# ScalarE in place of VectorE for the scaling of the delta-rule chunks, with a re-parameterised plan, in a two-layer hybrid encoder kernel

## The chip, the cores and the metric

The kernel runs on one core of a Trainium2 chip. A core has TensorE (matrix products and transposes into the eight banks of PSUM), VectorE and ScalarE (element-wise work, both can read PSUM), GpSimd (element-wise work in SBUF), and SyncE, whose queue here issues almost all transfers. In the profile they are PE (PEld for its weight loads), DVE, ACT, POOL and SP. The metric is the device time of one execution in microseconds.

## What is computed

Two layers over a sequence of 1024 rows of 1024 values. Each layer projects the normalised input with one wide matrix, runs three groups of mixers on it, and projects their gated results back:

```python
h = rmsnorm(x, pre_norm)
proj = jnp.einsum('bld,de->ble', h, w_in)
(gq, gk, gv, gz, gb, ga, sx, sB, sC, sz, sdt, rq, rk, rv, rg) = split_cols(proj, IN_SIZES)
qkv = jax.nn.silu(causal_conv(jnp.concatenate([gq, gk, gv], axis=-1), gdn_conv))
o_a = rmsnorm(gated_deltanet(...), gdn_norm) * jax.nn.silu(gz)        # 4 heads of 128
o_b = rmsnorm(ssd(...) * jax.nn.silu(sz), ssd_norm)                   # 16 heads in 2 groups
o_c = rmsnorm(retention(...), ret_norm) * jax.nn.silu(rg)             # 4 heads of 128
out = jnp.einsum('ble,ed->bld', jnp.concatenate([o_a, o_b, o_c], axis=-1), w_out)
return x + rmsnorm(out, post_norm)
```

The change touches the gated delta rule. For each head and each chunk it solves a triangular system and carries a state:

```python
sol = lax.linalg.triangular_solve(a_low + eye, rhs, left_side=True, lower=True)
u, w = sol[..., :GDN_DV], sol[..., GDN_DV:]
v_new = u - jnp.einsum('bhcd,bhdv->bhcv', w, S)
o = q_exp_gcum @ S + attn @ v_new
S = S * jnp.exp(glast) + jnp.einsum('bjhd,bhjv->bhdv', kdec, v_new)
```

## The kernel before

**Parts.** The work is done in four parts (p = 0 to 3): layer 0 on rows 0 to 511, layer 0 on rows 512 to 1023, then layer 1 likewise. Chunks have 128 rows here, four to a part.

**Projections.** The columns of w_in are cut into 26 pieces of 256 columns (PIECES), in this order: gates of the delta rule (gz), its q, k and v (gdn), B and C of the state-space group (bc), its gates and inputs for two groups (sz and sx), and retention (ret). Each piece has two halves of eight slices; a slice is 6 matmuls of 256 columns or 3 of 512. Every product is made of three, since a weight w is kept as a rounded high part and a low rest: hi x hi, lo x hi, hi x lo. ScalarE makes the high part (L2131), GpSimd the low one (L2417), four steps "split" for each piece. In the parts 0 and 2 all pieces are split, and those that are not in AGAIN are also stored as their two parts in w_split ("keep"), to be loaded as such in the parts 1 and 3. The pieces in AGAIN (0 to 3) are loaded raw and split again there. Two pieces are in SBUF at a time (W_RING).

**The delta rule.** For each head: transposes and the gram matrix (gdn_turn, gdn_gram), a forward substitution in blocks of 16 on VectorE (gdn_base, 16 parts, L1836 to L1856), then doubling steps gdn_p and gdn_xx for levels 4 to 6, each in two halves: a product on TensorE, then VectorE masks it into PP (L1888) or subtracts it from X (L1875, L1878). Then, for each of the four chunks, in a strict chain:
- gdn_s: TensorE multiplies keys and queries with the state; VectorE makes the residual (L1898), ScalarE scales the query part (L2252);
- gdn_v: TensorE multiplies the inverse with the residual; VectorE scales the result by row, from PSUM into vhat (L1903; its PSUM bank is then free);
- gdn_o: TensorE makes the state's increment and the output; VectorE updates the state (L1909, L1913).
gdn_open (transposes of v, q k products) and gdn_x0 (L1864) stand ahead of the first chunk, and gdn_fin1 to gdn_fin3 behind the last one: a sum (L1920), a gate product (L1924), squares on ScalarE (L2258), their mean (L1930, L1674), a power on GpSimd (L2375) and the last gate product (L1941). Then mix_turn transposes the head's result for the output projection.

**Output projection.** The mixed columns form 4 groups (delta rule, two state-space groups, retention) with 4 units each, of two steps "out" with 24 matmuls. For the parts 0 and 2 a unit's weights are split by ScalarE (L2156) and VectorE (L1976). The out steps of group 0 exist from the transposition of head 3 on; a group's transposition (mix_turn) is placed only when no older out step is left.

**The plan.** make_plan writes the order of all steps before the kernel is built. It keeps a clock for each engine with fixed costs (ACT and DVE 300 ns for such small steps, SLICE 705 ns), plays the steps on it, and at each point takes what is due: first a side step, a transposition, the next mixing step, the next doubling step, the next step ahead. These are taken if they are due by now + NEAR. If none is, an out unit goes if the next projection is late or stuck or if the next mixing step is more than OUT_WAIT away and APART slices lie behind the last one; else the next projection slice goes. All engines run their share of this one list in order, with semaphores between them, so an instruction that waits holds everything behind it on its engine. SyncE's list of transfers is sorted by the place in the plan of the step that releases each.

**What a piece must wait for (frees).** A gate piece writes one of two gate buffers: sz(1,0) needs mix_turn of heads 0 and 1, sz(1,1) that of heads 2 and 3. sx(0,*) writes a slot that head 2 read: it needs gdn_open of head 2, and its last half also head 2's last gdn_p. sx(1,*) needs gdn_open of head 3, its last half head 3's last gdn_xx.

Of the kernel before, what the change touches and what calls it, by code (L numbers as in the profile page):

```python
# [19 lines left out]
ALU = mybir.AluOpType  # L20
ACT = mybir.ActivationFunctionType
# [3 lines left out]
P = 128  # L25
# [6 lines left out]
GH, SH, RH = 4, 16, 4  # L32
# [14 lines left out]
PC = 256  # L47
N_GDN_PC, N_GZ, N_BC, N_SZ, N_SX, N_RET = 6, 2, 2, 2, 2, 8
PIECES = ([("gz", 0), ("gdn", 0), ("gdn", 1), ("gz", 1), ("bc", 0), ("gdn", 2), ("bc", 1), ("gdn", 3),
           ("sz", 0, 0), ("gdn", 4), ("sz", 0, 1), ("gdn", 5), ("sz", 1, 0), ("sx", 0, 0), ("sx", 0, 1), ("sx", 1, 0),  # L50
           ("sx", 1, 1), ("sz", 1, 1)]
          + [("ret", i) for i in range(N_RET)])
AT = {piece: i for i, piece in enumerate(PIECES)}
# [5 lines left out]


NTH = {m: n for n, m in enumerate(m_of(piece, half) for piece in PIECES if piece[0] in ("gdn", "bc", "sx") for half in range(2))}
AGAIN = range(4)
W_RING = 2
Q = KD
SBUF = 224 * 1024 - 1
# [172 lines left out]
def make_plan():  # L238
# [120 lines left out]
    def play(step):  # L359

        k, p = step[:2]
        r = step[2:]
        after = needs(step)
        pe = lambda w: run("pe", w, *after, "banks")
        dve = lambda w, *e: run("dve", w, *e)
# [3 lines left out]
        def mark(name, time):  # L369
            at[name] = time  # L370
# [13 lines left out]
        elif k == "split":  # L384
            n, j = len(PIECES) * p + r[0], r[1]
# [22 lines left out]
        elif k == "proj":  # L408
            i, half, q = r
            n = len(PIECES) * p + i  # L410
# [75 lines left out]
        elif k == "gdn_p":  # L486
            h, lv, j = r
# [8 lines left out]
        elif k == "gdn_xx":  # L496
            h, lv, j = r
# [6 lines left out]
            act(300, "n")  # L504
        elif k == "gdn_v":
            mark("n", pe(LINE) + 100)
            mark(("vhat", p, *r), dve(300, "n"))
        elif k == "gdn_o":
            mark("n", pe(LINE) + 100)
            mark(("gdn_oo", p, r[0]), pe(LINE) + 100)  # L510
# [40 lines left out]
        elif k == "ssd_y":  # L551
            g, c = r
# [162 lines left out]
    while mix_at < len(mix) or inv_at < len(inv) or pre_at < len(pre) or front_at < len(front) or outs or turns or any(sides.values()):  # L715
# [10 lines left out]
        step = mix[mix_at] if mix_at < len(mix) and known(mix[mix_at]) else None  # L726
# [42 lines left out]
def emptied_by_act(step, tag):  # L769

    k = step[0]
    return (k in ("small", "small2", "cum_turn", "x_turn") or k == "gdn_p" and tag != step
            or (k, tag[-1]) in (("gdn_turn", "q"), ("gdn_s", "q"), ("bc_turn", 0), ("ret_turn", "k")))


# [5 lines left out]
GATE_WAIT = 0  # L781
TABLE_WAIT = 1500
NORM_WAIT = 3000
OUT_WAIT = 4000
LATE = 200
SPLIT_FROM = 6
APART = 16
KEEP = 2
RELOAD = 4400
HOLD = 250  # L790
NEAR = 0
AHEAD = 2000
FAR = 1e12
SLICE, LINE, TURN, UNIT, TABLE, MB, LANDING = 705, 224, 109, 24 * 119, 1283, 3300, 2000
# [94 lines left out]
def no_state(step):  # L889

    return step[1] % 2 == 0 and step[3] == 0
# [42 lines left out]
def hybrid_kernel(nc, x, w_in, w_small, w_out, cons, rope, pars, rows, post_norm, out):  # L934
# [15 lines left out]
    with ExitStack() as ctx:  # L950
# [47 lines left out]
        sc = sb("sc", 2, 4, NT)  # L998
# [18 lines left out]
        resid, vhat = wk[:, 11, 0:2], wk[:, 11, 2:4]  # L1017
# [18 lines left out]
        small = flat[:, 3072:3072 + NT * NSM].rearrange("p (t n) -> p t n", t=NT)  # L1036
# [41 lines left out]
        def bank(tag):  # L1078
            return ps[:, bank_of[tag], :]
# [4 lines left out]
        def wait_filled(eng, tag):  # L1084
            eng.wait_ge(filled[bank_of[tag]], use_of[tag] + 1)
# [4 lines left out]
        def empty(ins, tag):  # L1090
            ins.then_inc(emptied[bank_of[tag]], 1)
# [52 lines left out]
        for n in range(PARTS * len(PIECES)):  # L1144
            p, i = divmod(n, len(PIECES))
# [4 lines left out]
        for n in range(PARTS * NT):  # L1150
            p, t = divmod(n, NT)
# [505 lines left out]
        def _(dve):  # L1657
# [8 lines left out]
            tt, ts, stt = nc.vector.tensor_tensor, nc.vector.tensor_scalar, nc.vector.scalar_tensor_tensor  # L1666
# [20 lines left out]
            for s in plan:  # L1687
                k, p = s[0], s[1]
                l, first_half = p // 2, p % 2 == 0
                if k == "norm":  # L1690
                    t = s[2]
                    for j in range(2):
                        tag = (*s, j)
# [8 lines left out]
                elif k == "small_turn":  # L1702
# [10 lines left out]
                    a, e, z, q, r, m = v  # L1713
# [18 lines left out]
                elif k == "proj":  # L1732
                    i, half, q = s[2], s[3], s[4]
                    tag = s[:4]
# [154 lines left out]
                elif k == "gdn_s":  # L1889
# [5 lines left out]
                    else:  # L1895
# [1 line left out]
                        wait_filled(dve, tag)  # L1897
                        empty(stt(resid[:, c % 2, :], bank(tag)[:, 0:P], dec[:, 0, c, h:h + 1], vb[:, c, :],  # L1898
                                  ALU.mult, ALU.subtract), tag)
                elif k == "gdn_v":  # L1900
                    h, c = s[2:]
                    wait_filled(dve, s)
                    empty(ts(vhat[:, c % 2, :], bank(s)[:, 0:P], sc[:, (GH * p + h) % 2, 0 if no_state(s) else 1, c:c + 1], None,  # L1903
                             ALU.mult), s)
                elif k == "gdn_o":
                    h, c = s[2:]
                    wait_filled(dve, s)
# [168 lines left out]
        def _(act):  # L2076
# [20 lines left out]
            for s in plan:  # L2097
# [24 lines left out]
                elif k == "split":  # L2122
# [6 lines left out]
                    if j == 2:  # L2129
                        act.wait_ge(w_in_sem[n % W_RING][1], loads_done(n))  # L2130
                    A(w_hi[:, n % W_RING, j * 512:(j + 1) * 512], wr[:, n % W_RING, j * 512:(j + 1) * 512], ACT.Copy)\  # L2131
                        .then_inc(S["w_hi_ready"], 1)
                elif k == "mix_turn" and s[2] == 0:
                    wait_filled(act, s)
                    A(mixT_hi[:, s[3], :], bank(s), ACT.Copy).then_inc(S["mix_hi"], 1)
# [334 lines left out]
```

## Time and profile before

| | before |
|---|---|
| median of 3 runs | 2117.5 us (2117.46 to 2117.93) |
| the profiled execution | 2121.16 us |
| its span, first to last instruction | 2119.2 us |
| TensorE busy | 2040.7 us (96%) |
| VectorE busy | 1453.5 us (69%) |
| ScalarE busy | 897.6 us (42%) |
| GpSimd busy | 525.3 us (25%) |
| mean granted clock of TensorE | 0.992 |

An engine is busy from an instruction's start to its end; matmuls overlap, and their ends are modelled. "A <- B" in a list of waits means that A stood still until B had ended. The granted clock is 1.00 at 2.4 GHz and 0.50 at 1.2 GHz. The mean granted clock is over the whole span, so 0.992 is a few short stretches at half the clock.

### The profile page before, as it was taken

To read this page: it belongs to the slowest core of one execution; us is meant where nothing else is said; L and a number is where in the kernel's file an instruction comes from. 1 tells how busy PE (TensorE), PEld (TensorE's weight loads), DVE (VectorE), ACT (ScalarE), POOL (GpSimd) and SP (SyncE) were. 2 spreads that over 40 slices of the span, in tenths; PEclk is the share of its full clock that TensorE was granted. 3 is DMA by queue.
4 is the path that set the end of the run, shared out by engine and by line. 5 is a ranking of instruction groups with operands and counts; after the bars stand their busy time and mean duration, and the time that the engine had idled before them with its cause. 6 is when DMAs were issued, how large, how long until landed. Compare 5 with 4: busy or idle time off the path is not lost.

```text
span 2119.2 us, 38332 instructions
## 1 busy us (share of the span) xinstructions
PE 2040.7 (96%) x14628; PEld 1880.3 (89%) x14628; DVE 1453.5 (69%) x3428; ACT 897.6 (42%) x1805; POOL 525.3 (25%) x464
## 2 busy tenths in 40 slices
PE   7998899999999999999999998899999999999997
PEld 6887888999889988899889897799988999899997
DVE  5888877756688787734578887775466877766334
ACT  5544376433533336412454344663335433474011
POOL 3433243333200101201243334433331001121001
PEclk9999999999999999999999999999999999999999
DMA  4554275666444565344355537556646445653424
GB/s 164 206 200 179 92 256 200 218 239 239 160 159 133 189 211 198 134 150 143 120 208 199 199 130 255 208 189 241 237 156 207 150 140 187 212 181 136 160 102 187
DMA packets 93589, 385.42 MB, mean 182 GB/s; under 512 B 10656, under 2 KB 11744, under 8 KB 81632
## 3 DMA queue, kind: packets, MB, share of 16 engines
q1 hardware_dynamic: 92832, 382.56, 51.6%
q8 instruction: 118, 1.93, 0.4%
q14 instruction: 63, 0.52, 0.1%
q10 hardware_dynamic: 576, 0.41, 0.1%
HBM read 248.55 MB, written 134.38 MB: 181 GB/s over the span
## 4 chain that ended last, share of the span: by engine, by line
PE 78%; DVE 9%; DMA 5%; issue 4%; ACT 3%; POOL 2%; SPq 0%; POOLq 0%; DVEq 0%; ACTq 0%
PE ps L1355 74%; PE ps L1358 4%; DMA w_split<-w_low 1%; POOL w_low L2417 1%; DVE base L1849 1%; DVE base L1848 1%; DMA wo_split<-wo_parts 1%; DVE slot L1747 1%; DMA wo_loaded<-in_w_out 1%; DMA w_loaded<-in_w_in 0%; DMA wo_parts<-wo_split 0%; DMA xfin<-x_mid 0%; DVE bc L1747 0%; DVE acc L2073 0%; DVE acc L1747 0%
## 5 line engine op out<-in xcount | busy, mean ns | idle before, releaser
L1355 PE MATMUL ps<-w_hi,hT_hi 128*128 128x256 f32 x1792 | 526.8, 294 | 11.0 <-POOL w_low L2417 9.1
L1355 PE MATMUL ps<-w_hi,hT_lo 128*128 128x256 f32 x1792 | 504.1, 281 | 0.0
L1355 PE MATMUL ps<-w_low,hT_hi 128*128 128x256 f32 x1792 | 502.6, 280 | 0.0
L2417 POOL TENSOR_TENSOR w_low<-w_loaded,w_hi 128x512 fp32r<-128x512 f32 x240 | 328.9, 1388 | 508.5 <-ACT w_hi L2131 508.5
L1355 PEld LDWEIGHTS ps<-w_hi,hT_hi 128*128 128x128 f32 x1792 | 338.7, 189 | 19.5 <-POOL w_low L2417 11.8
L1355 PEld LDWEIGHTS ps<-w_low,hT_hi 128*128 128x128 f32 x1792 | 339.0, 189 | 5.4 <-issue 4.8
L1355 PEld LDWEIGHTS ps<-w_hi,hT_lo 128*128 128x128 f32 x1792 | 340.1, 190 | 0.0
L1355 PE MATMUL ps<-hT_hi,w_hi 128*128 128x512 f32 x768 | 318.6, 415 | 5.3 <-POOL w_low L2417 5.3
L1355 PE MATMUL ps<-hT_lo,w_hi 128*128 128x512 f32 x768 | 304.3, 396 | 0.0
L1355 PE MATMUL ps<-hT_hi,w_low 128*128 128x512 f32 x768 | 303.8, 396 | 0.0
L1355 PE MATMUL ps<-wo_parts,mixT_hi 128*128 128x256 f32 x960 | 269.3, 281 | 0.0
L1747 DVE SCALAR_TENSOR_TENSOR slot<-raw,par,slot 128x512 f32<-128x512 f32 x222 | 191.8, 865 | 21.1 <-ACT slot L2203 11.1
L1990 DVE TENSOR_TENSOR acc<-acc,ps 128x512 f32<-128x512 f32 x96 | 65.7, 687 | 180.4 <-PE ps L1355 173.8
L1355 PEld LDWEIGHTS ps<-wo_parts,mixT_hi 128*128 128x128 f32 x960 | 181.5, 189 | 2.3 <-issue 1.4
L2131 ACT ACTIVATE w_hi<-w_loaded 128x512 fp32r<-128x512 f32 x240 | 139.4, 621 | 87.7 <-DMA w_loaded<-in_w_in 87.6
L1355 PEld LDWEIGHTS ps<-hT_lo,w_hi 128*128 128x128 f32 x768 | 144.7, 188 | 33.6
L1355 PEld LDWEIGHTS ps<-hT_hi,w_hi 128*128 128x128 f32 x768 | 145.3, 189 | 32.5 <-POOL w_low L2417 5.6
L1355 PEld LDWEIGHTS ps<-hT_hi,w_low 128*128 128x128 f32 x768 | 145.4, 189 | 25.8
L1355 PE MATMUL ps<-wk 128*128 128x128 f32 (+2 forms) x992 | 156.2, 290 | 9.9 <-issue 3.2
L1355 PEld LDWEIGHTS ps<-wk 128*128 128x128 f32 x992 | 134.2, 193 | 29.6 <-issue 13.7
L1355 PE MATMUL ps<-wo_hi,mixT_hi 128*128 128x256 f32 x480 | 138.4, 288 | 3.5 <-DVE wk L1814 2.0
L1355 PE MATMUL ps<-wo_hi_odd,mixT_hi 128*128 128x256 f32 x480 | 136.9, 285 | 1.2 <-DVE wo_parts L1976 1.1
(224 smaller groups left out, 3846.1 us busy)
## 6 DMA issues: line engine op xcount, KB each, us to landing
w_loaded<-in_w_in SPq DMA_DIRECT2D x120, 512.0 KB, 5.0
w_split<-w_hi SPq DMA_DIRECT2D x44, 1024.0 KB, 7.9
w_split<-w_low SPq DMA_DIRECT2D x44, 1024.0 KB, 10.0
w_hi<-w_split SPq DMA_DIRECT2D x88, 512.0 KB, 5.8
w_low<-w_split SPq DMA_DIRECT2D x88, 512.0 KB, 7.0
wo_loaded<-in_w_out SPq DMA_DIRECT2D x32, 512.0 KB, 4.3
wk<-cum_rows SPq DMA_DIRECT2D x32, 512.0 KB, 3.9
wo_split<-wo_parts SPq DMA_DIRECT2D x32, 512.0 KB, 7.8
```

Of the source, the lines that this page charges most:

```text
L1355: return nc.tensor.matmul(o, a, b, start=start, stop=stop)
L1358: return nc.tensor.transpose(o, a, ident)
L1747: stt(o, r[:, j:j + HALF], w[:, j:j + 1], o, ALU.mult, ALU.add).then_inc(S["conv_done"], 1)
L1848: chain(tt(step_t[:, :, i + 1:], copy_of(h, i)[:, :, i + 1:], cols_x[:, :, i:i + 1].broadcast_to([P, NT, n]), ALU.mult))
L1849: chain(tt(cols_x[:, :, i + 1:], cols_x[:, :, i + 1:], step_t[:, :, i + 1:], ALU.subtract))
L1990: empty(tt(o, o, b, ALU.add), s)
L2131: A(w_hi[:, n % W_RING, j * 512:(j + 1) * 512], wr[:, n % W_RING, j * 512:(j + 1) * 512], ACT.Copy)\
L2417: tt(w_lo[at], wr[at], w_hi[at], ALU.subtract)\
```

## The change

The scaling of gdn_v goes from VectorE's program to ScalarE's, as a Copy with the same column as scale, and the planner is told so (the bank is emptied by ScalarE). The pieces sx(0,0) and sx(0,1) go ahead of sz(1,0). Piece 0 leaves AGAIN: it is stored in parts 0 and 2 and loaded as two stored parts in parts 1 and 3. OUT_WAIT goes from 4000 to 1e9 ns and NEAR from 0 to 250 ns. The plan that comes out differs in the order of the steps; the arithmetic is the same.

```diff
--- before.py
+++ after.py
@@ -47,7 +47,7 @@
 PC = 256
 N_GDN_PC, N_GZ, N_BC, N_SZ, N_SX, N_RET = 6, 2, 2, 2, 2, 8
 PIECES = ([("gz", 0), ("gdn", 0), ("gdn", 1), ("gz", 1), ("bc", 0), ("gdn", 2), ("bc", 1), ("gdn", 3),
-           ("sz", 0, 0), ("gdn", 4), ("sz", 0, 1), ("gdn", 5), ("sz", 1, 0), ("sx", 0, 0), ("sx", 0, 1), ("sx", 1, 0),
+           ("sz", 0, 0), ("gdn", 4), ("sz", 0, 1), ("gdn", 5), ("sx", 0, 0), ("sx", 0, 1), ("sz", 1, 0), ("sx", 1, 0),
            ("sx", 1, 1), ("sz", 1, 1)]
           + [("ret", i) for i in range(N_RET)])
 AT = {piece: i for i, piece in enumerate(PIECES)}
@@ -59,7 +59,7 @@
 
 
 NTH = {m: n for n, m in enumerate(m_of(piece, half) for piece in PIECES if piece[0] in ("gdn", "bc", "sx") for half in range(2))}
-AGAIN = range(4)
+AGAIN = range(1, 4)
 W_RING = 2
 Q = KD
 SBUF = 224 * 1024 - 1
@@ -504,7 +504,7 @@
             act(300, "n")
         elif k == "gdn_v":
             mark("n", pe(LINE) + 100)
-            mark(("vhat", p, *r), dve(300, "n"))
+            mark(("vhat", p, *r), act(300, "n"))
         elif k == "gdn_o":
             mark("n", pe(LINE) + 100)
             mark(("gdn_oo", p, r[0]), pe(LINE) + 100)
@@ -769,7 +769,7 @@
 def emptied_by_act(step, tag):
 
     k = step[0]
-    return (k in ("small", "small2", "cum_turn", "x_turn") or k == "gdn_p" and tag != step
+    return (k in ("small", "small2", "cum_turn", "x_turn", "gdn_v") or k == "gdn_p" and tag != step
             or (k, tag[-1]) in (("gdn_turn", "q"), ("gdn_s", "q"), ("bc_turn", 0), ("ret_turn", "k")))
 
 
@@ -781,14 +781,14 @@
 GATE_WAIT = 0
 TABLE_WAIT = 1500
 NORM_WAIT = 3000
-OUT_WAIT = 4000
+OUT_WAIT = 1000000000.0
 LATE = 200
 SPLIT_FROM = 6
 APART = 16
 KEEP = 2
 RELOAD = 4400
 HOLD = 250
-NEAR = 0
+NEAR = 250
 AHEAD = 2000
 FAR = 1e12
 SLICE, LINE, TURN, UNIT, TABLE, MB, LANDING = 705, 224, 109, 24 * 119, 1283, 3300, 2000
@@ -1897,11 +1897,6 @@
                         wait_filled(dve, tag)
                         empty(stt(resid[:, c % 2, :], bank(tag)[:, 0:P], dec[:, 0, c, h:h + 1], vb[:, c, :],
                                   ALU.mult, ALU.subtract), tag)
-                elif k == "gdn_v":
-                    h, c = s[2:]
-                    wait_filled(dve, s)
-                    empty(ts(vhat[:, c % 2, :], bank(s)[:, 0:P], sc[:, (GH * p + h) % 2, 0 if no_state(s) else 1, c:c + 1], None,
-                             ALU.mult), s)
                 elif k == "gdn_o":
                     h, c = s[2:]
                     wait_filled(dve, s)
@@ -2130,6 +2125,10 @@
                         act.wait_ge(w_in_sem[n % W_RING][1], loads_done(n))
                     A(w_hi[:, n % W_RING, j * 512:(j + 1) * 512], wr[:, n % W_RING, j * 512:(j + 1) * 512], ACT.Copy)\
                         .then_inc(S["w_hi_ready"], 1)
+                elif k == "gdn_v":
+                    h, c = s[2:]
+                    wait_filled(act, s)
+                    empty(A(vhat[:, c % 2, :], bank(s)[:, 0:P], ACT.Copy, scale=sc[:, (GH * p + h) % 2, 0 if no_state(s) else 1, c:c + 1]), s)
                 elif k == "mix_turn" and s[2] == 0:
                     wait_filled(act, s)
                     A(mixT_hi[:, s[3], :], bank(s), ACT.Copy).then_inc(S["mix_hi"], 1)
```

## Rows read from the trace of the kernel before

**Rows 1.** The page: span, then busy time, share, instructions.
```profile
span 2119.2 us, 38332 instructions
...
PE 2040.7 (96%) x14628; PEld 1880.3 (89%) x14628; DVE 1453.5 (69%) x3428; ACT 897.6 (42%) x1805; POOL 525.3 (25%) x464
```

**Rows 2.** Waits of PE: who <- for whom: total us, times, longest.
```profile
PE ps L1355 <- POOL w_low L2417: 14.4, 12, 3.1
...
PE ps L1358 <- DVE gate L1941: 6.8, 2, 5.5
PE ps L1355 <- DVE wk L1875: 4.6, 2, 4.0
PE ps L1355 <- DVE slot L1888: 4.5, 5, 2.0
...
PE ps L1355 <- DVE st_g L1913: 3.3, 2, 1.9
PE ps L1355 <- DVE wk L1898: 2.9, 1, 2.9
PE ps L1355 <- DVE wk L1903: 2.4, 3, 1.4
```

**Rows 3.** Windows, busy us: four delta-rule stretches; parts 0 and 2, then sum.
```profile
106.00:300.00 194.00, 177.71 (x1114) 156.84 (x1113) 161.81 (x446) 87.64 (x179) 69.10 (x55) 0.97 0.48 171
...
1143.00:1344.00 201.00, 182.59 (x1206) 163.55 (x1206) 167.12 (x422) 85.76 (x179) 76.92 (x62) 0.97 0.55 195
...
sum 754.00, PE 714.00 PEld 643.03 DVE 607.90 ACT 302.11 POOL 181.15; mean PE 178.50 PEld 160.76 DVE 151.97 ACT 75.53 POOL 45.29
```

**Rows 4.** Groups by form, DVE then ACT: busy us, mean ns | idle before.
```profile
L1903 DVE TENSOR_SCALAR wk<-ps,sc 128x128 f32<-128x128 f32 x64 | 22.2, 348 | 11.7 <-PE ps L1355 10.8
...
L2252 ACT ACTIVATE wk<-ps,dec 128x128 f32<-128x128 f32 x56 | 20.4, 364 | 81.5 <-PE ps L1355 80.9
```

**Rows 5.** Waits of PE between 190 and 222 us.
```profile
PE ps L1355 <- DVE wk L1875: 4.0, 1, 4.0
...
PE ps L1358 <- DVE wk L1864: 1.3, 1, 1.3
```

**Rows 6.** Windows of short stretches; PEclk stands after POOL's busy time.
```profile
217.20:220.60 3.40, 3.40 (x17) 3.40 (x17) 3.37 (x8) 0.60 (x1) 0.00 (x0) 0.50 0.00 0
...
1340.20:1347.00 6.80, 3.75 (x18) 3.75 (x19) 4.22 (x5) 6.77 (x18) 3.90 (x4) 0.50 0.02 8
...
1551.80:1555.20 3.40, 3.40 (x19) 3.40 (x18) 0.67 (x1) 2.46 (x6) 0.74 (x2) 0.50 0.00 0
```

**Rows 7.** Timeline of DVE and PE at 1342 us: start, us, instruction [idle before].
```profile
1341.70 1.50 DVE L1941 TENSOR_TENSOR gate<-gate,ss 128x512 f32<-128x512 f32 x1
...
1343.25 1.12 PE L1358 MATMUL ps<-con,gate 128*128 128x128 f32 x4 [5.47 <-DVE gate L1941]
```

**Rows 8.** Timeline of ACT and PE at the first piece of part 3.
```profile
1548.08 1.06 ACT L2105 ACTIVATE junk<-wk 128x1024 f32<-128x1024 f32 x1 [9.06 <-DMA wk<-x_mid]
...
1549.13 0.61 ACT L2131 ACTIVATE w_hi<-w_loaded 128x512 fp32r<-128x512 f32 x1
...
1551.42 0.38 PE L1355 MATMUL ps<-w_hi,hT_hi 128*128 128x256 f32 x1 [2.78 <-POOL w_low L2417]
```

**Rows 9.** Timeline: two chunks whose scaling came late on DVE.
```profile
167.80 0.46 PE L1355 MATMUL ps<-wk 128*128 128x128 f32 x2 [0.48 <-DVE wk L1878]
...
173.40 0.34 DVE L1903 TENSOR_SCALAR wk<-ps,sc 128x128 f32<-128x128 f32 x1
...
1777.37 1.70 ACT L2156 ACTIVATE wo_hi_odd<-wo_loaded,par 128x256 fp32r<-128x256 f32 x4 [8.33 <-DMA wo_loaded<-in_w_out]
...
1779.51 0.34 DVE L1903 TENSOR_SCALAR wk<-ps,sc 128x128 f32<-128x128 f32 x1
```

**Rows 10.** DMA issues: tensor, queue, count, KB each, median us to landing.
```profile
w_split<-w_low SPq DMA_DIRECT2D x44, 1024.0 KB, 10.0
```

## What the change does to the time, predicted

> **What bounds the kernel now.** The page comes first: TensorE is busy for 2040.7 us of a span of 2119.2 us [rows 1], and its total work isn't touched by the change. So the change can only act on the 78.5 us between (2119.2 - 2040.7), on gaps too short to be counted as idle, and on the clock. The second view says who holds TensorE up [rows 2]: GpSimd's low halves of the weights for 14.4 us, and VectorE for most of the rest, namely the gate product of L1941 (6.8 us) and the steps of the delta-rule chain (L1875 4.6, L1888 4.5, L1913 3.3, L1898 2.9, L1903 2.4 us). L1903 is the instruction that moves. The reader should see there that its own wait is 2.4 us in three places; all that the move can give beyond that comes from the room that it leaves on VectorE. The third view cuts out the four stretches in which the chain of the four delta-rule heads runs: VectorE is busy for 161.81 of 194 us in the first part of the sequence and 167.12 of 201 us in the third, 83% both, ScalarE for 45% and 43%, and TensorE idles for 16.3 and 18.4 us [rows 3]. That is where a VectorE instruction is worth something. In the other two parts the sum leaves TensorE only 5.3 us of idleness. The fourth view is the granted clock: three of the kernel's slow stretches, at half the clock (0.50, the 1.2 GHz level against 2.4 GHz), come right at the end of such a wait [rows 6].
>
> **The moved instruction.** 64 instructions at 348 ns leave VectorE: 22.2 us [rows 4]. The form that comes to ScalarE (Copy with a scale from a 128x1 operand, 128x128 out of PSUM) is there already as L2252, at 364 ns and without a table load: 64 x 0.364 = 23.3 us, on an engine with more than half of each stretch free. On the chain of a head each chunk gets 16 ns longer, 1.0 us in all if none is covered. The Trainium skill speaks against this edit: "ScalarE: Activation LUTs", section Rules for kernel authors, gives a multiply to VectorE, and its figure for an ACTIVATE with one 128x1 operand comes to 386 ns for 128 elements. By that the chain would grow by 64 x 38 ns = 2.4 us instead of 1.0 us; the row for the very form says 364 ns and decides.
>
> Waiting in line is the larger matter. On VectorE the scaling often waits behind other work: one matmul of this step began at 167.80 us, and its scaling at 173.40 us [rows 9]. On ScalarE it will stand behind conversions of weights, some of which wait for a transfer, with the gate and convolution evictions of the next projection behind it in turn; if it comes late, they do, and through them the two banks of the projections. At 1777.37 us ScalarE had sat 8.33 us waiting for a transfer, and VectorE, waiting for ScalarE's result, reached the scaling at 1779.51 us only [rows 9]: in such a place neither engine is the better one. I take the time in line as equal, with 5 us less or more as bounds. What is left is the room on VectorE: 22.2 of 607.9 busy us, 3.7% [rows 3]. The waits for L1888, L1913, L1898 and L1903 add up to 13.1 us [rows 2]; nothing is gone if each is a matter of order, 6.5 us if half is a matter of load. I take a fifth, -2.6 us, with the 1.0 us above: **-1.6 us**.
>
> **The order of the pieces.** Today sz(1,0) comes before sx(0,0) and sx(0,1). It writes the ring of gates that head 1's result leaves only with its turn (frees), so projections stop until head 1 is done. In the first part no out units exist yet to fill in, and TensorE waits 1.3 us for L1864 and 4.0 us for L1875 [rows 5]. Right after it comes a stretch at half the clock from 217.2 to 220.6 us in which TensorE is busy throughout: 1.7 us lost [rows 6]. sx(0,0) needs only gdn_open of head 2, and L1864 reads what that step wrote, so both waits lie behind it: after the change sx(0,0) can fill them, with 16 slices of the planner's 705 ns, 11 us of matmuls. Its convolution puts VectorE work into the same place, which delays the chain, but covered by projections. **-7.0 us**; bounds 0 (the stop moves to the next blocked piece) and -7.0.
>
> **The end of head 3 in the third part.** Here the last gate piece sz(1,1) waits for head 3: TensorE stands 5.47 us at 1343.25 us for L1941, which ends the chain of head 3 [rows 7], and then runs at half the clock up to 1347 us, with 3.75 us of busy time in that window, 1.9 us of it lost [rows 6]. The reordering doesn't add work to fill this place with; only a shorter chain does. 16 scalings of this part take 5.6 us off VectorE, about the size of the wait, but not all of them are on the path. Half: **-3.7 us**, bounds 0 and -7.4.
>
> **Piece 0 is split once (AGAIN).** In parts 1 and 3 the first piece is loaded as stored halves. Eight conversions on ScalarE and eight subtractions on GpSimd fall away. In part 3 this removes a wait: ScalarE sat 9.06 us for x_mid, the conversion queued behind it began at 1549.13 us, and TensorE went on at 1551.42 us after 2.78 us [rows 8], then at half the clock until 1555.2, 1.7 us [rows 6]. **-4.5 us**. Part 1 has no such wait. What is added: in parts 0 and 2 two stores of 1 MB after the first piece, and in parts 1 and 3 twice the bytes of the load. A store lands after 10.0 us [rows 10], and the load into the same ring slot has to wait for it, with everything behind it in SP's queue. Bounds: 0 and +5 us (half of a store, for each of two parts 2.5 us). I take 0, since the store is issued one half piece ahead of the load's own release and the slot's next piece is used one piece later.
>
> **NEAR from 0 to 250.** The planner may now put a chain step where its data is due up to 250 ns later, instead of one more slice of projection (705 ns) before it. A step whose due time falls anywhere in the last slice is brought forward in 250/705 = 0.355 of the cases and TensorE then waits 125 ns on average. Chain steps: 96 of gdn_p and as many of gdn_xx, 64 each of gdn_v and gdn_o, 56 of gdn_s, 64 of ret_o and 32 of ssd_y, 472 in all, counts by the loops, with those of gdn_v (L1903) and gdn_s (L2252) in [rows 4]. 472 x 0.355 x 0.125 = 20.9 us if each stands behind a slice. Many follow another chain step directly, so I take less than half, **+9 us**. Bounds +0 and +21. The gain in return (each chain a little earlier) is in the terms above. OUT_WAIT at 1e9 lets out units go only where projections are late or stuck or no mixing step is known; it saves them as filler for the stops and costs nothing by itself: 0, bounds -3 and +3.
>
> **Sum.** -1.6 - 7.0 - 3.7 - 4.5 + 9.0 = -7.8 us. The profiled execution took 2121.2 us, of which 2119.2 are span; it would take 2113.4. The median of the plain runs is 3.7 us lower, and 2117.5 - 7.8 = 2109.7 us.
>
> **Rivals.**
> (1) The stops move. The filling work is the same in all; projections used up beside head 1 are missing beside head 3, and the 7.0 us come back at sz(1,1) of the first part. For it: that is what the third part shows at 1343 us. Against it: in the first part sz(1,1) isn't delayed today. 2109.7 + 7.0 = 2116.7 us.
> (2) Slower: the slots opened by NEAR become waits. The planner charges 300 ns for the scaling, where rows show 348 and 364 ns [rows 4], and likewise for its neighbours, so a step put 250 ns before its planned due time waits for more than that. Place: everywhere a chain step stands behind a slice, in all four parts and in the retention steps too, where nothing is won. Price 20.9 us in place of 9, and 2.5 us more for the stores in each of two parts, against gains of 16.8 us without the half of the third part's 3.7: 2117.5 + 20.9 + 5 - 15.0 = 2128.4 us at the worst, 2123.4 without the stores. It decides from 16.8 us on, that is a mean wait of 36 ns over the 472 steps (I take 19).
> (3) VectorE's load is the true bound of the stretches with 83%: the third part's wait goes whole (-7.4), half of the 13.1 us goes too (-6.5 + 1.0), and NEAR costs half (+4.5): 2117.5 - 7.0 - 7.4 - 4.5 - 5.5 + 4.5 = 2097.6 us.
> (4) It doesn't do what it says: excluded for the move itself, which is one instruction for another; for OUT_WAIT it may be so, since it matters only where a mixing step is known and over 4 us off.
>
> **How the numbers follow.** Forecast (2103 to 2113): 0.48. Rival (3): 0.12. Rival (1) and everything else that ends within 0.2% (4.2 us, about what a measurement of this kernel can tell from no change): 0.22. Rival (2): 0.18. So faster 0.60, same 0.22, slower 0.18. The range goes from rival (3) to between the two values of rival (2): 2097 to 2126; below it I leave 0.06 and above it 0.08.
>
> **What the profile after would show.** ScalarE has 64 more instructions near 364 ns and VectorE 64 fewer; VectorE's busy time falls from 1453.5 us [rows 1] to about 1431. No waits for L1864 or L1875 around 210 us and no slow clock at 217 us. No wait for GpSimd's w_low at the first piece of part 3. The wait for L1941 in part 3 halved or gone. TensorE's waits, in number, rise (many of 0.1 to 0.3 us, "issue" or VectorE). Wrong if: a wait of over 3 us for L1941 stands in the first part (rival 1), the many small waits add up to over 17 us (rival 2), or new waits for the scaling on ScalarE, behind conversions that wait for transfers, exceed the 2.4 us that TensorE waits for it on VectorE.

## The result, and the profile after

The changed kernel takes 2147.2 us (median of 4 runs, 2143.98 to 2151.15) beside 2117.5 us: 1.0136 times as long, interval 1.0123 to 1.0149. That is 30 us slower, outside the range and on the other side of the forecast.

The page of the profiled execution after (span 2146.3 us), answering to [rows 1]:

```profile
PE 2054.7 (96%) x14628; PEld 1884.4 (88%) x14628; DVE 1430.0 (67%) x3364; ACT 911.7 (42%) x1859; POOL 510.1 (24%) x456
```

Work has moved as forecast: VectorE is at 1430.0 us (1431 forecast), with 64 instructions fewer. TensorE's matmuls are the same, and its busy time is 14 us longer. Its waits after, answering to [rows 2] (engine <- for whom: total us, times, longest; the lines behind the edit have moved up by one to five, so L1936 is L1941 of before):

```profile
PE ps L1355 <- issue: 20.6, 5, 9.4
PE ps L1358 <- DVE gate L1936: 9.8, 2, 5.0
...
PE ps L1355 <- DVE slot L1888: 8.0, 5, 3.2
PE ps L1355 <- POOL w_low L2416: 6.6, 9, 2.2
PE ps L1355 <- DVE wk L1875: 3.2, 5, 1.3
...
PE ps L1355 <- ACT wk L2131: 2.8, 2, 1.9
```

GpSimd's halves, 14.4 us before, cost 6.6; the moved scaling (L2131 now) costs 2.8 us where it had cost 2.4. New is the first row, 20.6 us of "issue", 17.6 us of it in two stops, of 8.2 and 9.4 us. Here is the first, in the timeline of PE, ACT and SP at the end of part 0 (start, us, instruction, [idle before <- releaser]):

```profile
513.31 2.04 PE L1355 MATMUL ps<-wk 128*128 128x128 f32 x8 [8.19 <-issue]
```
```profile
508.94 1.06 ACT L2100 ACTIVATE junk<-wk 128x1024 f32<-128x1024 f32 x1 [12.09 <-DMA wk<-in_x]
...
511.04 1.15 ACT L2104 ACTIVATE wk<-wk,xrs 128x1024 f32<-128x1024 f32 x1 [0.95 <-POOL xrs L2352]
512.09 0.36 ACT L2220 ACTIVATE slot<-ps 128x256 f32<-128x256 f32 x1
512.35 0.37 ACT L2221 ACTIVATE gate<-ps 128x256 f32<-128x256 f32 x1
512.62 0.60 ACT L2314 ACTIVATE wk<-ps 128x512 f32<-128x512 f32 x1
```
```profile
490.13 0.32 SPq L1288 DMA_DIRECT2D w_hi<-w_split  x1
490.49 0.43 SPq L1289 DMA_DIRECT2D w_low<-w_split  x1
490.97 0.43 SPq L1288 DMA_DIRECT2D w_hi<-w_split  x1
491.44 0.43 SPq L1289 DMA_DIRECT2D w_low<-w_split  x1
491.92 0.67 SPq L1297 DMA_DIRECT2D wo_split<-wo_hi  x1
492.63 0.64 SPq L1298 DMA_DIRECT2D wo_split<-wo_parts  x1
493.31 0.58 SPq L1292 DMA_DIRECT2D w_split<-w_hi  x1
493.93 0.63 SPq L1293 DMA_DIRECT2D w_split<-w_low  x1
497.06 1.21 SPq L1232 DMA_DIRECT2D wk<-in_x  x2
```

Read them from the bottom. SyncE issues 2 MB of the stored piece 0 (its halves; before, 1 MB raw), then four stores (two of 0.5 MB to wo_split and two of 1 MB to w_split, 3 MB together), and only then two tiles of x for part 1. ScalarE has reached the squares of such a tile and waits 12.09 us. In line behind it stand two evictions and the copy of the last retention head's keys (L2314, done at 513.2). TensorE's next matmuls, ret_s(0,3), read that copy. So "issue" stands here for a wait two steps away: TensorE waits for ScalarE, and ScalarE for a transfer. The same picture stands at the start of part 3: 13.34 us of waiting for x_mid on ScalarE, 9.44 us on TensorE at 1568.86. The clock fell in both. The rows of windows (length, PE, PEld, DVE, ACT, POOL busy, PEclk, DMA share, GB/s):

```profile
510.33:513.70 3.37, 0.39 (x2) 0.42 (x3) 0.00 (x0) 2.66 (x5) 0.59 (x2) 0.50 0.54 216
513.70:517.16 3.46, 3.46 (x19) 3.46 (x18) 0.69 (x1) 2.31 (x4) 0.74 (x2) 0.50 0.01 2
1561.60:1571.80 10.20, 2.94 (x14) 2.97 (x15) 0.69 (x1) 5.42 (x10) 1.49 (x4) 0.50 0.54 189
```

Outside the first and last 20 us, the clock is at 0.50 for 27 us before and for 44 us after. The waits of 190 to 222 us [rows 5] are gone, but at the end of head 3 there is now a stop in part 0 as well as in part 2 (timeline of PE, two places):

```profile
298.79 1.12 PE L1358 MATMUL ps<-con,gate 128*128 128x128 f32 x4 [4.97 <-DVE gate L1936]
```
```profile
1352.61 1.12 PE L1358 MATMUL ps<-con,gate 128*128 128x128 f32 x4 [4.83 <-DVE gate L1936]
```

A sum over all matmul records, worked out for this text, sorts the delays. For the first matmul of each step other than a projection or an out unit, I take the time since the matmul before it began, less the usual time for such a pair (the tenth percentile of all kernels' records of it at full clock). The last column is the time at a granted clock of 0.50 outside the first and last 20 us:

| kernel | delays under 1 us, sum | over 1 us, sum | at 0.50 |
|---|---|---|---|
| before | 10.8 us | 25.9 us | 27 us |
| after | 22.3 us | 46.7 us | 44 us |
| after with NEAR 0 (e2_near0, below) | 12.4 us | 30.2 us | 48 us |
| after with late stores (f3_stores_late) | 21.9 us | 30.5 us | 24 us |

These sums depend on what is called usual. A second count, with the usual time taken apart for each pair of steps and of tiles, gives 9.7, 22.5, 9.4 and 22.2 us under 1 us and 25.5, 44.5, 27.7 and 28.3 us over it. By that count the short delays are 19 to 25 us in all six kernels of this document with NEAR at 250, and 6 to 14 us in all fourteen with NEAR at 0.

### The profile page after: what moved, and what is told of

It is laid out like the page before. It is cut to its first block and busy times, and to the rows that moved or that the text cites. A ratio compares the mean times of both kernels' runs of the same rounds, so it can differ in the third digit from the quotient of the medians.

```text
span 2146.3 us, 38311 instructions
## 1 busy us (share of the span) xinstructions
PE 2054.7 (96%) x14628; PEld 1884.4 (88%) x14628; DVE 1430.0 (67%) x3364; ACT 911.7 (42%) x1859; POOL 510.1 (24%) x456
## 5 line engine op out<-in xcount | busy, mean ns | idle before, releaser
L2416 POOL TENSOR_TENSOR w_low<-w_loaded,w_hi 128x512 fp32r<-128x512 f32 x232 | 316.9, 1382 | 477.6 <-ACT w_hi L2126 477.4
L1747 DVE SCALAR_TENSOR_TENSOR slot<-raw,par,slot 128x512 f32<-128x512 f32 x222 | 186.2, 840 | 21.7 <-ACT slot L2204 10.0
L1355 PE MATMUL ps<-wk 128*128 128x128 f32 (+2 forms) x992 | 159.7, 294 | 29.6 <-issue 20.6
```

Source lines behind the costliest of these rows:

```text
L1355: return nc.tensor.matmul(o, a, b, start=start, stop=stop)
L1747: stt(o, r[:, j:j + HALF], w[:, j:j + 1], o, ALU.mult, ALU.add).then_inc(S["conv_done"], 1)
L2416: tt(w_lo[at], wr[at], w_hi[at], ALU.subtract)\
```

## The experiments

Each is a change of before or after. Where a setting of the planner is changed, the plan comes out anew; where it says so, the plan is kept. A ratio is to the kernel before as measured beside the run (medians from 2118.9 to 2119.3 us), with its 95% interval. Where two runs are compared in us, the difference is that of their medians, and each median is good to some 2 us, with four executions to 4.

### Which part costs

**after with AGAIN as before.**
```diff
-AGAIN = range(1, 4)
+AGAIN = range(4)
```


> The changed kernel with AGAIN back at pieces 0 to 3, the plan made anew. Theory A: piece 0 is loaded raw again, 1 MB instead of 2 MB ahead of the x tiles at the start of parts 1 and 3; the two waits shrink to what the kernel before shows (0 and 2.8 us), 2125 to 2131 us. If the x tiles' place in ScalarE's order alone makes the wait, it stays near 2147. Theory B and C: 2147 within 4 us (plus or minus what another plan gives).

2136.1 us, 1.0082 of before (1.0063 to 1.0100): 11 us faster than after, where theory A had 16 to 22. The two long stops are 3.9 and 2.9 us.

**after with NEAR as before.**
```diff
-NEAR = 250
+NEAR = 0
```


> The changed kernel with NEAR back at 0, the plan made anew. Theory B: the many small waits go, 2147 - 20 = 2127 us or less. Theory A: only as far as ret_s of head 3 is placed later; the waits under 0.25 us sum to little in the trace of the changed kernel (about 3 us more than before), so 2140 to 2147 us.

2116.4 us, 0.9987 (0.9977 to 0.9998): 31 us faster than after, in theory B's range. The two long stops are gone, and the small delays are back at 12.4 us. The clock is at 0.50 for 48 us here, as long as in after, so the 31 us aren't the clock's.

**after, its plan kept, scaling back on VectorE** (the branch of gdn_v goes back to VectorE's program, with the same bank order).

> The changed kernel with its plan unchanged, the 64 scalings alone moved back to VectorE. Theory C (ScalarE delays them): 2147 - 15 to - 25 us. Theory A and B: 2147 within 4 us; slower by up to 5 us if the room on VectorE was worth something.

2163.5 us, 1.0211 (1.0196 to 1.0227): 16 us slower than after: theory C is refuted, and the loss is more than the 5 us that the other theories allowed. TensorE's first row of waits in this run:

```profile
PE ps L1355 <- DVE wk L1903: 21.0, 17, 3.1
```
So the move is a gain on this plan, and what after loses against before isn't ScalarE's doing.

**before with NEAR 250 and nothing else.**

> The kernel before with NEAR at 250 in place of 0 and nothing else, the plan searched anew. Theory 1 (the allowance is the part that costs, by itself, with VectorE scaling as in before): 15 to 35 us slower than before, 2132 to 2152, and many small waits for VectorE, as in the run with the scaling moved back (20 us of waits on the scaling's line). Theory 2 (the allowance costs only together with the second kept first piece, whose transfers stand before the x tiles): within 5 us of before, since the kernel before keeps no first piece. The long stop ahead of ret_s(0,3) near 510 us tells too: under 1 us by theory 2, over 4 us by theory 1.

2144.1 us, 1.0114 (1.0098 to 1.0130), 25 us. No long stop at 510 us, so the size is that of theory 1 and the sign of the stop that of theory 2. The small delays are 21.1 us. Stops of 6.6 us at 219 and 4.0 at 1794 us are new, and one of 3.1 us at 1305 has grown to 4.4 at 1307. NEAR needs no other edit to cost 25 us. The two long stops of after aren't there, so on this plan the 25 us must be the short delays and other stops.

### What the two long stops are made of

**after, one step of ScalarE moved.** The scaling of x tile 2 is placed behind ret_turn(p,3), the step of which L2314 is ScalarE's part.
```diff
+    for p in (0, 2):
+        for step in (("rescale", p + 1, 2), ("scale", p + 1, 2)):
+            plan.remove(step)
+            plan.insert(plan.index(("ret_turn", p, 3)) + 1, step)
```


> The changed kernel with its own plan, except that in parts 0 and 2 the squares and the scaling of the next part's third x tile stand behind ret_turn of head 3 instead of ahead of it, so that ScalarE makes the key copy for ret_s before it waits for that tile. Theory A (ScalarE waits 12 us for an x tile whose load stands behind 5 MB of other transfers, and ret_s of head 3 stands behind it): the two PE waits of 8.3 and 9.6 us go, with the slow clock behind them, 2147 - 18 - 4 = 2125 us, or a few us more if the third tile's own norm is late then. Theory B (NEAR costs 20 us everywhere) and theory C (the scaling waits in line on ScalarE): within 3 us of 2147.

2134.9 us, 1.0077 (1.0060 to 1.0093), 12 us faster than after, where theory A had 22. The stops shrink to 2.0 and 3.5 us and stand now at norm, the step that needs the tile itself.

**after, the plan kept, stores behind the x tiles** in SyncE's list.
```diff
-                loads.append((where["proj", p, i, 0, Q - 1], n, ("keep", p, i)))
+                at = where["proj", p, i, 0, Q - 1]
+                if i == len(PIECES) - 1:
+                    at = max(at, where["norm", p + 1, 1] + 0.5)
+                loads.append((at, n, ("keep", p, i)))
```
(and likewise for the "keep_unit" that falls there)

> The changed kernel; on SyncE's queue the stores of kept weights that stand ahead of the loads of x tiles 2 and 3 of parts 1 and 3 (3 MB at each of the two places) are issued behind these two loads; the plan and all engines' orders stay. Theory 1 (the two long stops are the transfer of the x tile behind the kept data, which holds ScalarE's order and with it the evictions behind it): both stops shrink by what the stores took, 4 to 8 us each, so 8 to 14 us faster than after, 2133 to 2139. Theory 2 (the x tile's own load is long, whatever is ahead, or the load of the next first piece, which stays ahead, is what it waits for): under 3 us faster than after, and the waits of ScalarE for the x tile stay near 12 us.

2129.7 us, 1.0060 (1.0039 to 1.0081), 17.5 us faster than after (by the two ratios 16 us, good to 5), at or above the upper end of theory 1's 8 to 14. SyncE and ScalarE at the same place:

```profile
497.10 1.21 SPq L1238 DMA_DIRECT2D wk<-in_x  x2
498.35 0.43 SPq L1303 DMA_DIRECT2D wo_split<-wo_hi  x1
```
```profile
501.77 1.06 ACT L2106 ACTIVATE junk<-wk 128x1024 f32<-128x1024 f32 x1 [4.88 <-DMA wk<-in_x]
```
The load is issued at the same time (497.10 and 497.06), and the tile is used 7.2 us earlier (501.77 and 508.94). Four stores, 3 MB together, are all that was taken from ahead of it. Between 497 and 508.9 us the transfers of after moved 396 GB/s, by which 3 x 1048576 bytes take 7.9 us, an estimate. The Trainium skill ("DMA: Bandwidth & Descriptors", section Where 436 GB/s comes from) puts SBUF's sixteen ports together at 435 GB/s and says that the memory's side, about 358 GB/s for a core, binds for transfers between HBM and SBUF; by these figures the 3 MB take 7.2 or 8.8 us, both estimates. The trace's 396 GB/s is above the second figure, and the 7.2 us measured are nearest to the first. The windows of the place show what it was worth (TensorE busy of 20 us, first after, then this run):

```profile
1555.00:1575.00 20.00, 10.56 (x80) 10.39 (x79) 5.53 (x15) 6.12 (x10) 1.49 (x4) 0.74 0.61 237
```
```profile
1555.00:1575.00 20.00, 20.00 (x174) 20.00 (x174) 14.72 (x35) 4.47 (x9) 4.83 (x4) 1.00 0.41 133
```
The plan and all engines' orders are the same in both kernels, so the stores are shown as the cause of the two long stops. What is left to NEAR 0 is 13.3 us (2129.7 - 2116.4). The delays under 1 us are 9.5 us of it by the table and 12.8 us by the second count; that they are the rest of the cost is read from the traces, and no run takes them away alone.

**after with NEAR 0 and the first piece raw again.**

> The changed kernel with NEAR 0 and AGAIN over all four parts (the first piece of a layer's second part loaded raw again), both as in before, with the piece order, the OUT_WAIT and the scaling on ScalarE as in after. After with NEAR 0 was 31 us faster than after, after with AGAIN over four 11 us faster. Theory 1 (both act through the same stop at the x tile at the start of parts 1 and 3): with NEAR 0 that stop was gone already, so AGAIN adds nothing: 2113 to 2119. Theory 2 (the two costs are separate): 31 + 11 off 2147, 2105 or so.

2116.9 us, 0.9992 (0.9983 to 1.0001): theory 1, as with the piece kept (2116.4).

**after with NEAR 0 and the stores late.**

> The changed kernel with NEAR 0, and the stores of kept weights at the ends of parts 0 and 2 behind the loads of the next x tiles, as in the run where that gave 17 us off the changed kernel. Theory 1 (at NEAR 0 the x tile is late too, only less: kept first piece and stores eat the gain of the kept piece): 3 to 8 us faster than the run with NEAR 0 alone (2116.4), 2109 to 2113. Theory 2 (at NEAR 0 nobody waits for that tile at TensorE, since ret_s is placed behind more slices): 2115 to 2118. By theory 2 the cost of the kept first piece exists only together with the early placing of ret_s.

2116.3 us, 0.9987 (0.9978 to 0.9996): theory 2. In after with NEAR 0 and the stores in their old place, ScalarE waits 4.4 us for the x tile, and TensorE doesn't stand at all there. Two things differ from after. Its plan has four slices between ret_turn(0,3) and ret_s(0,3), where after has one. And only 2 MB of stores stand ahead of the tile's load, which is used 8.0 us behind its issue in place of 11.9. So the kept piece and the stores cost only on the plan that NEAR 250 makes; which of the two differences does more isn't shown.

### The move by itself

**before, its plan kept, scaling on ScalarE.**

> The kernel before with one edit: ScalarE does the 64 scalings out of PSUM, every other instruction and its order stays. Theory 1 (the move is worth what TensorE waited for VectorE's scaling, as forecast): 1.6 us less than before, 2116 to 2118, and no more waits on the scaling's line. Theory 2 (the move is worth as much here as on the plan of after, where taking it back cost 16 us): about 2103. Theory 3 (ScalarE's order, which this plan was not made for, puts the scaling behind longer work of ScalarE): slower than before by up to 5 us, with TensorE's wait on the new ScalarE line over 4 us in sum.

2122.0 us, 1.0018 (1.0008 to 1.0028): slower by 3 us, theory 3. TensorE waits for the scaling more than it did when VectorE made it (2.4 us in 3 places [rows 2]):

```profile
PE ps L1355 <- ACT wk L2131: 6.6, 7, 2.2
```

**the same with the plan made anew for it** (before with ScalarE in code and planner).

> The kernel before with ScalarE scaling and the planner's cost moved to ScalarE too, so the plan is searched anew for that alone (old piece order, AGAIN, NEAR, OUT_WAIT). With the old plan this move gave 2122. Theory 1 (the plan had been the reason for that loss: ScalarE's order put the scaling behind longer work): 2112 to 2118, TensorE's waits for the new ScalarE line under 3 us. Theory 2 (the move costs by itself when VectorE is not late): 2120 to 2124.

2137.5 us, 1.0089 (1.0075 to 1.0102): neither theory; 15 us worse than with the plan left alone. Its waits for L2131 are 7.7 us, its mean clock is 0.982 (before 0.992), and it has stops of over 3 us at 213, 219, 822, 1289, 1359 and 1798 us.

**after with NEAR 0 and AGAIN over four, the plan kept, scaling on VectorE.**

> The changed kernel with NEAR 0 and AGAIN over four parts (2116.9 with the scaling on ScalarE), its exact plan kept, the 64 scalings done by VectorE. On the plan of after this cost 16 us, on the plan of before ScalarE cost 3. Theory 1 (a plan made for ScalarE's scaling has VectorE's chain packed so that the scaling no longer fits, whatever NEAR is): 8 to 16 us slower, 2125 to 2133. Theory 2 (only with NEAR at 250, where steps are placed with no slack, does VectorE's extra 22 us show): 2117 to 2121.

2148.7 us, 1.0139 (1.0121 to 1.0158), against 2116.9 with the scaling on ScalarE: 32 us, twice the most that theory 1 expected.

```profile
PE ps L1355 <- DVE wk L1903: 26.2, 15, 5.7
```
The 5.7 us in VectorE's timeline:
```profile
179.71 0.67 DVE L1808 TENSOR_REDUCE gss<-junk 128x4 f32<-128x512 f32 x1
...
181.10 1.11 DVE L1824 SCALAR_TENSOR_TENSOR slot<-ps,sc,et 128x128 f32<-128x128 f32 x4
182.13 0.34 DVE L1903 TENSOR_SCALAR wk<-ps,sc 128x128 f32<-128x128 f32 x1
```
The scaling takes 0.34 us and stands behind the preparation of the next head (L1808 to L1824). The plan had put that there with the scaling on ScalarE in view.

### Pieces and OUT_WAIT

**before with the new piece order alone** (the first diff of the change).

> The kernel before with the new order of pieces and nothing else (scaling on VectorE, first piece kept only as before, NEAR 0, OUT_WAIT 4000), the plan searched anew. Theory 1 (the forecast: the 7 us of stops in front of gdn turns near 209 to 217 us of part 0 go and nothing comes back): 2112 to 2114. Theory 2 (the stops only change their place; two stops of about 4 us near 225 and 300 us take over, as the runs with NEAR 0 and the new order show them): 2117 to 2122.

2127.3 us, 1.0043 (1.0031 to 1.0056), above both theories' ranges. The waits of 190 to 222 us are gone here too, and part 1 begins (its first projection slice) at 497.7 us in place of 508.7; but part 2 begins at 1013.0 in place of 1012.3, and part 3 at 1556.8 in place of 1546.3. The eleven microseconds are given back in part 1, and ten more are lost in part 2; part 3 is 4 us shorter.

**before with OUT_WAIT at 1e9 alone.**

> The kernel before with OUT_WAIT at 1e9 in place of 4000 and nothing else, the plan searched anew. The forecast priced this edit at nothing (3 either way); with the new piece order and the scaling on ScalarE it was worth 21 us (2138.2 to 2116.9). Theory 1 (the setting is a gain of its own, through the order of the output units): faster than before too, 2100 to 2110. Theory 2 (it makes good what the other edits broke, and before had nothing to make good): 2117 to 2125. Theory 3 (each new search lands elsewhere, and the kernel before stands at a place found by trying): over 2125.

2121.2 us, 1.0018 (1.0009 to 1.0027): 2 us slower, in theory 2's range.

**new piece order and scaling on ScalarE, OUT_WAIT 4000** (NEAR 0, AGAIN over four).

> The changed kernel with NEAR 0, AGAIN over four parts and OUT_WAIT 4000, that is the kernel before with the new piece order and the scaling moved in code and plan. Beside the run that differs in OUT_WAIT alone (2116.9). Theory 1 (OUT_WAIT is worth nothing, as forecast): 2114 to 2120. Theory 2 (output units held back for stretches without front work fill waits better): 3 to 6 us slower, 2120 to 2123.

2138.2 us, 1.0095 (1.0080 to 1.0110), against 2116.9 with OUT_WAIT at 1e9: neither theory. The profiled executions are 16 us apart. Two groups of waits are 19.2 us longer together, GpSimd's low halves 5.5 us longer, and others are shorter:

```profile
PE ps L1355 <- DVE wk L1875: 10.5, 4, 5.0
PE ps L1358 <- ACT gate L2308: 10.3, 2, 6.0
```
With 1e9 they are 1.0 and 0.6 us.

**as the run of 2116.9, old piece order.**

> The changed kernel with NEAR 0, AGAIN over four parts and the old piece order: it differs from the run of 2116.9 in the piece order alone, and from the run of 2137.5 in OUT_WAIT alone. Theory 1 (edits add up: OUT_WAIT gives 21 here too, and the order of pieces nothing or a few us): 2114 to 2120. Theory 2 (they don't add up): anything from 2120 to 2140; then no edit of this change has a price of its own, only the four with the setting together.

2137.5 us, 1.0097 (1.0083 to 1.0112): theory 2, the edits don't add up. With NEAR 0 and AGAIN over four, the three remaining edits give:

| scaling, pieces | OUT_WAIT 4000 | OUT_WAIT 1e9 |
|---|---|---|
| VectorE, old | 2119 (before) | 2121.2 |
| VectorE, new | 2127.3 | not run |
| ScalarE, old | 2137.5 | 2137.5 |
| ScalarE, new | 2138.2 | 2116.9 |

OUT_WAIT is worth 2 us of loss, nothing, or 21 us of gain.

### Stops taken away by hand

**before, mix_turn(2,0,3) behind six slices of sz(1,1)** in place of ahead of them; the rest of the plan is kept.
```diff
+    step = ("mix_turn", 2, 0, 3)
+    plan.remove(step)
+    plan.insert(plan.index(("proj", 2, len(PIECES) - N_RET - 1, 0, 5)) + 1, step)
```


> The kernel before, its plan kept but for one step: the turn of head 3 of part 2 (mix_turn(2,0,3), at which TensorE stood 5.5 us at 1343) is done behind the first six slices of the piece that follows, in place of ahead of them. Theory 1 (that stop is an order in which TensorE waits with work at hand, as the forecast took it): stop under 1 us and no slow clock behind it, 5 to 7 us faster, 2112 to 2114. Theory 2 (the step behind is late as well, so the wait moves on): 2117 to 2120.

2115.6 us, 0.9990 (0.9982 to 0.9999), 3.3 us faster than before beside it by the medians and 0.2 to 3.8 us by the ratio, between the two theories. The stop of 5.47 us [rows 7] is 1.24, and the slow clock behind it is gone. Windows of before and of this run:

```profile
1335.00:1355.00 20.00, 14.53 (x102) 13.34 (x101) 13.34 (x20) 12.66 (x28) 4.88 (x4) 0.83 0.33 118
```
```profile
1335.00:1355.00 20.00, 16.63 (x124) 14.32 (x123) 16.29 (x24) 14.98 (x35) 5.47 (x5) 1.00 0.56 201
```

**the same step on the plan of 2116.9.**

> The changed kernel with NEAR 0 and AGAIN over four parts (2116.9), with the same single step moved: its stop there was 4.2 us at 1344. Theory 1: 4 to 6 us faster, 2111 to 2113, faster than both kernels. Theory 2 (the wait moves on): 2115 to 2118.

2117.2 us, 0.9994 (0.9985 to 1.0003). The stop of 4.2 us is gone, the time isn't: theory 2 for the time, though the trace shows no new stop of that size. In one profile the span is 2.6 us shorter, which plain runs don't bear out; this stays open.

**before with three stops reordered** (that step, gdn_base(0,2,14) behind gdn_v(0,1,3), and turn, gram and rs of head 3 behind gdn_p(0,2,5,1) in part 0).

> The kernel before with steps of its own plan moved at three stops: mix_turn(2,0,3) as in the run where it gave 3.3 us, gdn_base(0,2,14) behind gdn_v(0,1,3) (1.1 of the 2.9 us at 202), and gdn_turn, gdn_gram, gdn_rs of (0,3) and gdn_base(0,3,0) behind gdn_p(0,2,5,1), since their work on VectorE (213.0 to 216.8) stands ahead of the L1883 copies that TensorE waits for 4.0 us at 217. Theory 1 (waits made by VectorE's order, so an order that does the awaited result first takes them away): the stop at 217 under 2 us, with the clock 3 to 6 us off the run with the mix turn alone (2115.6), 2110 to 2113. Theory 2 (VectorE is the bound in this stretch, so the wait moves on to the next head's inverse): 2114 to 2117.

2115.1 us, 0.9983 (0.9974 to 0.9993): theory 2, and no faster than the run with the mix turn alone (2115.6) by more than the noise. The stop at 217 us went, one of 2.6 us at 211 came in its place, and that of 2.9 at 202 stayed. TensorE in the window, before and then this run:

```profile
195.00:225.00 30.00, 19.88 (x125) 18.16 (x123) 25.35 (x73) 6.59 (x12) 5.29 (x5) 0.83 0.30 106
```
```profile
195.00:225.00 30.00, 21.70 (x140) 20.20 (x139) 26.08 (x76) 7.75 (x15) 6.00 (x6) 0.83 0.31 106
```
VectorE is busy for 26 of 30 us and TensorE for 1.8 us more than before. That fits theory 2, by which VectorE bounds this stretch and another order gives little. It isn't shown: in before with the scaling on ScalarE and the plan kept (b_act), the stops of 2.9 and 4.0 us stand unchanged, but only a few scalings lie ahead of them there.

## Why the prediction was wrong, step by step

**NEAR (+9.0).** This is the term that was furthest off. For what it priced, short waits ahead of chain steps, it was near: 22.3 - 12.4 = 9.9 us by the table, 13 us by the second count. That is partly luck, since "less than half of 20.9" was a guess with no row behind it. The step that failed is what it left out: it took the wait of an early step to be 125 ns, and a longer one to be worth nothing. A step placed early isn't only waited for a little. The instruction that releases it may be an instruction of ScalarE that stands behind a transfer, and then the wait is the transfer's. The planner has no clock for this one: it marks x_in, the landing of an x tile, for part 0 alone. That is 17.5 us by the late stores, and the setting's whole price here is 31 us in place of 9. Rival (2) had the sign but 19 us too little (2128.4), and only half of its mechanism: the small waits are there, at half to two thirds of the 20.9 us it gave them, and the rest is stops of 1 to 9 us.

**AGAIN (-4.5, cost taken as 0).** The wait at the first piece of part 3 went, as forecast. The cost failed: I looked at the ring slot and the bank of the next load, and not at what stands behind in SyncE's list, the x tiles, though their 9.06 us wait was in [rows 8]. With NEAR 250 the edit costs 11 us, with NEAR 0 nothing either way. The term of -4.5 us was no gain in the time of either.

**The order of pieces (-7.0).** The mechanism was right and the balance wrong: part 0 gets 11 us shorter in the run of that edit alone, more than forecast, and the whole 8 us longer. Rival (1) happened (a stop of 4.97 us at sz(1,1) of part 0 in after, 5.4 at 295 us in the run alone), and the further losses lie in parts 1 and 2, where I had priced nothing.

**Head 3 in part 2 (-3.7).** 4.83 us are left of 5.47. "Half, from a lighter VectorE" failed: in b_act, with the plan kept and the 16 scalings off VectorE, 5.24 us are left too. What also failed is the sentence that nothing can fill this place. The planner asks for the free gate buffer at every slice of the piece, but in the kernel only ScalarE's eviction behind the last slice of a half waits for it (L2212 of the kernel before). So six slices stood at hand, and one step moved by hand took the stop away. It gave 3.3 us of the 7.4 that the forecast had as the bound, and nothing on the plan of 2116.9.

**The move (-1.6).** Durations were right (median 367 ns against 364). The room on VectorE was sized well: in b_act the waits for L1888, L1913 and L1898, 10.7 us before, are 8.6, and those for the scaling itself went from 2.4 to 6.6 us. "Time in line taken as equal" is what failed, and in a way that no value could have mended: the same exchange of engines is 3 us of loss on the plan made for VectorE, and 16 and 32 us of gain on two plans made for ScalarE. What it is worth isn't a property of the instruction but of the order that it stands in. An order made anew for it is no remedy either: from before, that cost 18 us. The Trainium skill's figures ("ScalarE: Activation LUTs", section What ACT_TABLE_LOAD costs) come to 386 ns for the moved instruction, an estimate; the trace's 367 ns is below it.

**OUT_WAIT (0, 3 either way).** Right alone (+2), wrong by 21 us beside the others.

**The signs of being wrong.** All three came, and only the first two weigh. A wait of 4.97 us for the last gate product stands in part 0. The small waits add up to 22 us, over 17, though before had 11 of them already. The waits for the scaling on ScalarE are 2.8 us, over 2.4.

**The sum.** This is the failure above the others: the terms were read off stops of the old plan, as if the plan stayed and only these places changed. Each setting makes a new order. Four edits were tried on before one at a time with a new plan: pieces cost 8 us, ScalarE 18, NEAR 25 and OUT_WAIT 2; none gained. AGAIN was not tried on before alone. The chance of slower, 0.18, should have carried that. Why each new order is worse by its own stops is shown only for those named here.

## What to carry to other kernels

When an edit makes a planner choose a new order, don't sum what it does to the stops of the old order: ask what the planner's clock doesn't model (here the x tiles of the later parts), and price the case that a step lands behind that. Before a load or a store is added, read the queue's list beyond it, down to the next transfer that an engine with work in line behind it waits for. A stop in which TensorE waits with free slices at hand can be moved by hand with the rest of the order kept; here that took two such stops away, and gave 3.3 us on one plan and nothing on the other. Each change of engine is worth measuring with the order kept and with it made anew.

## What the runs showed of the hardware

The same load, issued at 497.06 us in one kernel and at 497.10 us in the other, was used at 508.94 and at 501.77 us, with and without 3 MB of stores issued ahead of it on the same queue: a store that nobody waits for delays a load that somebody does. And the granted clock fell at long stops, not under the many short delays: it was 0.50 from 510.33 to 517.16 us across and behind a stop of 8.2 us, and 0.83 on average over 1335 to 1355 us with the stop of 5.47 us, where with 1.24 us of waiting in its place it was 1.00. After and the run with late stores have the same 22 us of short delays, and outside the first and last 20 us they run for 44 and 24 us at 0.50. The time at 0.50 doesn't tell the time of a kernel, though: after with NEAR 0 has 48 us of it, with fewer long delays than after (30.2 us against 46.7), and is 31 us faster.
